# Two value projections as 512-column products, in slabs of four contraction tiles

## The chip, the cores and the metric

The kernel runs on one core of a Trainium2 chip. The metric is the device time of one execution in microseconds (us), given as the median of several runs. The core has five engines that run their own instruction streams and meet only at semaphores: TensorE (PE in the profile; PEld is its weight load), VectorE (DVE), ScalarE (ACT), GpSimd (POOL), and SyncE (SP), which here only issues DMAs.

## The reference

Two transformer blocks on 512 tokens of width 1024, in float32. The change touches only the first block, and there two of the eleven pieces of one input projection:

```
h = rmsnorm(x, g_mix_pre)
proj = h @ w_in                                  # 512 x 1024 times 1024 x N_IN
aq, ak, av, iq, ik, iw, bq, bk, bv, cq, gate_logits = split(proj)
ya = dsa_attention(aq, ak, av, iq, ik, iw, rel_bias) @ w_up_a
yb = stick_breaking_attention(bq, bk, bv) @ w_up_b
yc = memory_attention(cq, mk, mv) @ w_up_c
merged = gates[0]*ya + gates[1]*yb + gates[2]*yc
x = x + rmsnorm(merged @ w_out)
x = x + rmsnorm((silu(h2 @ Wg) * (h2 @ Wu)) @ w_ffn_out)   # h2 = rmsnorm(x)
# then a second block: chunkwise mLSTM layer, dilated window attention, two gated additions
```

`av` and `bv` are both 512 x 512: the value rows (512 tokens by 8 heads of 64). In `dsa_attention` a score per query and key is formed from `iq`, `ik`, `iw`; the 128 best keys of each query are selected, and a softmax over those (8 heads, causal by chunks of 64) weighs the rows of `av`. In `stick_breaking_attention` the weights of `bv`'s rows are exp(log_sigmoid(z) + the sum of log_sigmoid(-z) over later keys).

The kernel runs the three attentions in the order `memory_attention` (the first attention below), `dsa_attention` (the second), `stick_breaking_attention` (the third).

## The kernel before

**Weights in slabs.** All weights come through two slots, each of 2048 words per partition. Slab number g uses slot g mod 2. For each slab SP loads it (`raw`), ScalarE writes a rounded copy (`w_hi`, L1474), GpSimd writes the remainder (`w_lo = raw - w_hi`, L559, or in four quarters, L579), and TensorE multiplies. `split_hi(stage, s)` on ScalarE makes `w_hi` of the slab *after* slab s of the stage; it waits until the slab two before that one has been used. Every product is three matmuls into one accumulator (`mm3`, L734): hi x hi, hi x lo, lo x hi. The stages and the number of slabs of each stand in one table (L50); the semaphore counts `EV_A[stage]` and `EV_V[stage]` say how many evacuations by ScalarE and by VectorE come before a stage.

**The order around the change** is ... `aqk` (4 slabs), `av` (2), `bqk` (4), `bv` (2), `gate` (24). It is written out by hand on each engine. There is no scheduler.

**A 256-column slab** (`gemm_rows`, L853) holds all eight contraction tiles of 256 output columns. With the tokens as the stationary side it makes 4 row tiles x 8 contraction tiles x 3 = 96 matmuls of 256 columns, into two PSUM banks (two row tiles to a bank): banks 0 and 1 for slot 0, banks 2 and 3 for slot 1. When the slab is used up, ScalarE empties one bank and VectorE the other (`to_rows`), each with one 128x512 instruction.

**A wide slab** (`gemm_wide`, L825; used so far only in the second block, by `v2`, `o2` and others) holds four contraction tiles of 512 columns. Two slabs make a group of 512 columns: in the first, all four row tiles take k = 0 to 3, in the second k = 4 to 7, each row tile in a bank of its own. That is 48 matmuls of 512 columns a slab. A row tile is complete only in the second slab; `wait_tile` lets an engine wait for row tile t there (`tile_done`, and `slab_used` for the last one).

**VectorE before the second attention** (L2203 to L2216). VectorE selects the best keys with 96 instructions (`select`, MAX8 and MATCH_REPLACE8 in turn), 20 ahead of each of five evacuations (`aqk` 1 to 3, `av` 0 and 1), but 16 ahead of the last. After the last of them it writes the masks (L2213), then waits for and empties `av` 1. GpSimd waits for the masks (`mask_made`), then writes the offsets (bias plus mask) of unit 0, 1, 2, ... (L644). A unit is one head and one row tile: 32 units.

**The second attention, step by step.** In step n, VectorE forms the negated logits of unit n with their minimum (L2225; needs offset n), and normalises unit n - 1. ScalarE copies transposed probabilities and takes the exponentials of unit n (L1567). TensorE forms the logits of units n and n + 1 in each even step (`pair_logits`, L994), which waits until both logits of the pair before have been read by VectorE (`at_neg`). It fills each of steps 0 to 31 with two of the products of `bqk` (six matmuls, `products_beside`). In step n it transposes unit n - 3 and, in odd steps, multiplies by `av`. ScalarE splits slab 1 of `bqk` at the end of step 1. GpSimd writes its `w_lo` in four quarters, one after each of offsets 2 to 5 (L640 to L648). In steps 33 to 35 TensorE fills with row tile 0 of `bv` (`first_rows_of_bv`, L1021).

**The third attention.** TensorE finishes slab 0 of `bv`, then row tile 0 of slab 1, then the first logits of head 0 (`first_stick_z`), then the rest of slab 1, then the logits of head 1, and so on, one head per step (L1101 to L1132). Head 0 uses banks 2 to 4, head 1 banks 5 to 7, in turn. In step 0, ScalarE and VectorE empty slab 1 of `bv` after their work for head 0.

Of the kernel before, what the change touches and what calls it, by code (L numbers as in the profile page):

```python
# [22 lines left out]
ACT = mybir.ActivationFunctionType  # L23
# [3 lines left out]
P = 128  # L27
S = 512
NT = S // P
D = 1024  # L30
KD = D // P
SLAB = 2048
HALF = 512
# [69 lines left out]

WIDE = {"v2": 2, "o2": 2, "z2": 2, "wout2": 2, "pg0": 2, "kv3": 2, "q3": 3, "wout3": 2, "pg1": 2}
GROUPS = {**{n: 1 for n in WHOLE}, **WIDE}
GROUP_NO = {}
# [119 lines left out]
def _program(nc, A, ctx):  # L226
# [178 lines left out]
    def slot_of(tensor, slot, words=SLAB):  # L405
        return tensor[:, slot * SLAB:slot * SLAB + words]

    def wait_tile(eng, stage, t, c=0):

        if t < NT - 1:  # L410
            eng.wait_ge(tile_done, (NT - 1) * (GROUP_NO[stage] + c) + t + 1)
        else:
            eng.wait_ge(slab_used, BASE[stage] + COUNT[stage] // GROUPS[stage] * (c + 1))
# [23 lines left out]
    def _(sp):  # L437
# [65 lines left out]
        load("aqk", columns(w_in, C_AQ))  # L503
        load("av", columns(w_in, C_AV))
        load("bqk", columns(w_in, C_BQ))
        load("bv", columns(w_in, C_BV))

# [222 lines left out]
    def _(pe):  # L730
# [93 lines left out]

        def gemm_wide(stage, c, x_hi, x_lo, half, kt=KD, ready=None, bank_free=None, between=None, after_tile=None):  # L825

            per = kt // 4
            for s in range(per):
                g = BASE[stage] + per * c + s
                pe.wait_ge(lo_made, g + 1)  # L830
                hi, lo = (slot_of(w, g % 2).rearrange("p (k c) -> p k c", k=4) for w in (w_hi, w_lo))
                if s and between is not None:
                    between()
                for t in range(NT):
                    if s == 0 and bank_free is not None:
                        bank_free(t)
                    for k in range(4 * s, 4 * s + 4):
# [3 lines left out]
                        ins = mm3(banks[:, 4 * half + t, :], x_hi[:, at_], x_lo[:, at_], hi[:, k % 4, :], lo[:, k % 4, :], k == 0, k == kt - 1)  # L841
# [149 lines left out]
        gemm_T("aqk", h_hi, h_lo, first=1, count=3)  # L991
        gemm_rows("av", h_hi, h_lo)

        def pair_logits(n):  # L994

            pe.wait_ge(at_neg, U_A + n)
            for m in (n, n + 1):
                h, t = head_and_tile(m)
                rows = slice(64 * (m % 2), 64 * (m % 2) + 64)
                w = (t + 1) * P  # L1000
                mm(banks[:, 4 + m % 2, 0:w], aqkT[rows, (h // 2) * S + t * P:(h // 2) * S + (t + 1) * P],
                   aqkT[rows, (4 + h // 2) * S:(4 + h // 2) * S + w], True, True).then_inc(at_log, 1)
# [18 lines left out]
        def first_rows_of_bv(k0, k1):  # L1021

            slot = wait_slab("bv", 0, 0, 0)
            hi, lo = (slot_of(w, slot).rearrange("p (k c) -> p k c", k=KD) for w in (w_hi, w_lo))
            for k in range(k0, k1):
                mm3(banks[:, 2 * slot, 0:256], h_hi[:, k * S:k * S + P], h_lo[:, k * S:k * S + P], hi[:, k, :], lo[:, k, :], k == 0, k == KD - 1)
# [64 lines left out]
        def first_stick_z():  # L1091

            pe.wait_ge(at_lo, 8)
            pe.wait_ge(ev_a, EV_A["bv"] + 1)
            pe.wait_ge(ev_v, EV_V["bv"] + 1)
# [352 lines left out]
    def _(act):  # L1448
# [248 lines left out]
        for step in range(8 + 2):  # L1697
# [310 lines left out]
    def _(dve):  # L2008
# [180 lines left out]
        n_select = 2 * (NT - 1) * TOPK // 8  # L2189

        def select(n):

# [10 lines left out]
        n_now = 0  # L2203
        to_empty = [("aqk", s, to_T(aqkT, scale=0.125 if s < 2 else 1.0)) for s in range(1, 4)] + [("av", s, to_rows(av, HALF)) for s in range(2)]
        share = -(-n_select // len(to_empty))
        for n, (stage, s, empty) in enumerate(to_empty):
# [3 lines left out]
            if n_now == n_select:  # L2210
# [23 lines left out]

        each_slab("bv", to_rows(bv, HALF), 0, 1)
        dve.tensor_copy(sums_r[:], sq[:, SQ["ntri"] * P:(SQ["ntri"] + 2) * P]).then_inc(sums_made, 1)
        for step in range(8 + 2):
# [385 lines left out]
```

## Time and profile before

| | us |
|---|---|
| median of 3 runs | 1555.07 (1554.88 to 1556.66) |
| span of the profiled execution, first to last instruction | 1553.7 |
| what the median is above that span | 1.4 |
| PE busy | 1529.0 (98%) |
| DVE, ACT, POOL busy | 703.0, 601.9, 693.8 |

The profile lists no time of the profiled execution apart from its span. TensorE is busy in nearly the whole span and the other four less than half of it. Start times in the rows are microseconds from the start of the span. A matmul's listed duration is its latency: with matmuls in a row, the distance between two starts is what each one costs.

### The profile page before, as it was taken

To read this page: it belongs to the slowest core of one execution; us is meant where nothing else is said; L and a number is where in the kernel's file an instruction comes from. 1 tells how busy PE (TensorE), PEld (TensorE's weight loads), DVE (VectorE), ACT (ScalarE), POOL (GpSimd) and SP (SyncE) were. 2 spreads that over 40 slices of the span, in tenths; PEclk is the share of its full clock that TensorE was granted. 3 is DMA by queue.
4 is the path that set the end of the run, shared out by engine and by line. 5 is a ranking of instruction groups with operands and counts; after the bars stand their busy time and mean duration, and the time that the engine had idled before them with its cause. 6 is when DMAs were issued, how large, how long until landed. Compare 5 with 4: busy or idle time off the path is not lost.

```text
span 1553.7 us, 19713 instructions
## 1 busy us (share of the span) xinstructions
PE 1529.0 (98%) x7588; PEld 1253.4 (81%) x7588; DVE 703.0 (45%) x1147; ACT 601.9 (39%) x916; POOL 693.8 (45%) x312
## 2 busy tenths in 40 slices
PE   8999999999999999999999999999999999999898
PEld 7777967877888888888888888888888888887687
DVE  4258855482334226665654005630034346444733
ACT  6353254673332225122221115422444444355452
POOL 6423455334555535443434444444432435454532
PEclk9999999999999999999999999999999999999999
DMA  7314211102333332433332225543422322222021
GB/s 246 122 55 136 82 55 49 41 21 61 102 101 87 109 109 70 118 97 104 85 108 86 104 82 72 99 104 92 126 68 72 101 89 82 95 82 82 28 72 64
DMA packets 145126, 138.26 MB, mean 89 GB/s; under 512 B 7792, under 2 KB 118384, under 8 KB 145052
## 3 DMA queue, kind: packets, MB, share of 16 engines
q1 hardware_dynamic: 140836, 130.79, 29.3%
q10 hardware_dynamic: 4216, 6.45, 1.3%
q8 instruction: 51, 0.84, 0.2%
q14 instruction: 23, 0.19, 0.0%
HBM read 135.09 MB, written 2.13 MB: 88 GB/s over the span
## 4 chain that ended last, share of the span: by engine, by line
PE 90%; DVE 3%; ACT 3%; POOL 2%; issue 1%; DMA 0%; ACTq 0%; DVEq 0%; POOLq 0%
PE banks L732 87%; PE banks L761 2%; POOL w_lo L579 1%; PE banks L920 1%; PE banks L1350 0%; DVE prob L2552 0%; DVE xs L2072 0%; ACT w_hi L1474 0%; POOL prob L721 0%; DMA vec_rows<-in_norm_a 0%; ACT junk L1523 0%; ACT k L1938 0%; POOL prob L723 0%; ACT junk L1762 0%; DVE head_ms L2514 0%
## 5 line engine op out<-in xcount | busy, mean ns | idle before, releaser
L559 POOL TENSOR_TENSOR w_lo<-raw,w_hi 128x2048 fp32r<-128x2048 f32 x104 | 481.4, 4629 | 602.3 <-ACT w_hi L1474 602.3
L732 PE MATMUL banks<-h_hi,w_hi 128*128 128x512 f32 (+1 forms) x904 | 348.1, 385 | 2.4 <-DVE h_lo L2079 0.9
L732 PE MATMUL banks<-h_hi,w_lo 128*128 128x512 f32 (+1 forms) x904 | 340.4, 377 | 0.0
L732 PE MATMUL banks<-h_lo,w_hi 128*128 128x512 f32 (+1 forms) x904 | 340.1, 376 | 0.0
L1474 ACT ACTIVATE w_hi<-raw 128x2048 fp32r<-128x2048 f32 (+2 forms) x123 | 233.1, 1895 | 213.3 <-PE banks L732 203.1
L732 PEld LDWEIGHTS banks<-h_hi,w_hi 128*128 128x128 f32 x904 | 169.9, 188 | 42.1 <-issue 9.7
L732 PE MATMUL banks<-w_hi,h_hi 128*128 128x512 f32 (+1 forms) x544 | 199.8, 367 | 0.0
L732 PE MATMUL banks<-w_hi,h_lo 128*128 128x512 f32 (+1 forms) x544 | 198.2, 364 | 0.0
L732 PE MATMUL banks<-w_lo,h_hi 128*128 128x512 f32 (+1 forms) x544 | 198.1, 364 | 0.0
L732 PEld LDWEIGHTS banks<-h_hi,w_lo 128*128 128x128 f32 x904 | 169.6, 188 | 32.2
L732 PEld LDWEIGHTS banks<-h_lo,w_hi 128*128 128x128 f32 x904 | 169.9, 188 | 29.5
L579 POOL TENSOR_TENSOR w_lo<-raw,w_hi 128x512 fp32r<-128x512 f32 x84 | 113.6, 1373 | 104.3 <-ACT w_hi L1474 92.1
L732 PEld LDWEIGHTS banks<-w_hi,h_hi 128*128 128x128 f32 x544 | 102.6, 189 | 16.9 <-issue 1.1
L732 PEld LDWEIGHTS banks<-w_hi,h_lo 128*128 128x128 f32 x544 | 102.6, 189 | 16.2
L732 PEld LDWEIGHTS banks<-w_lo,h_hi 128*128 128x128 f32 x544 | 102.7, 189 | 15.8
L2351 DVE TENSOR_TENSOR f_lo<-ff_prod,f_hi 128x512 f32 x22 | 104.2, 4738 | 2.7
L1794 ACT ACTIVATE ff_sig<-banks 128x512 f32<-128x512 f32 x22 | 13.2, 600 | 175.9 <-PE banks L732 175.9
L732 PE MATMUL banks<-w_hi,f_lo 128*128 128x512 f32 x176 | 68.5, 389 | 0.0
L732 PE MATMUL banks<-w_hi,f_hi 128*128 128x512 f32 x176 | 68.5, 389 | 0.0
L732 PE MATMUL banks<-w_lo,f_hi 128*128 128x512 f32 x176 | 68.5, 389 | 0.0
L1735 ACT ACTIVATE gate<-banks,col 128x512 f32<-128x512 f32 x24 | 16.6, 690 | 130.5 <-PE banks L732 130.5
L2060 DVE TENSOR_REDUCE meansq<-sumsq 128x1 f32<-128x2 f32 (+4 forms) x19 | 2.9, 153 | 139.3 <-ACT junk L1762 130.4
(319 smaller groups left out, 2348.6 us busy)
## 6 DMA issues: line engine op xcount, KB each, us to landing
raw<-in_w_in SPq DMA_DIRECT2D x56, 512.0 KB, 4.0
raw<-in_w_ffn_in SPq DMA_DIRECT2D x44, 512.0 KB, 5.0
raw<-in_w_in_a SPq DMA_DIRECT2D x32, 512.0 KB, 5.7
raw<-in_w_ffn_out SPq DMA_DIRECT2D x22, 512.0 KB, 4.0
raw<-in_w_ple_gate SPq DMA_DIRECT2D x16, 512.0 KB, 4.6
raw<-in_w_in_b SPq DMA_DIRECT2D x16, 512.0 KB, 4.5
raw<-in_w_out SPq DMA_DIRECT2D x8, 512.0 KB, 4.0
raw<-in_w_out_a SPq DMA_DIRECT2D x8, 512.0 KB, 4.5
```

The source lines that it names most:

```text
L559: pool.tensor_tensor(slot_of(w_lo, slot), slot_of(raw, slot), slot_of(w_hi, slot).bitcast(F32), ALU.subtract).then_inc(lo_made, 1)
L579: ins = pool.tensor_tensor(w_lo[:, c], raw[:, c], w_hi[:, c].bitcast(F32), ALU.subtract)
L732: return pe.matmul(out, lhsT, rhs, start=start, stop=stop, **kw)
L761: ins = pe.transpose(banks[:, transposed_bank(name, k), t * P:(t + 1) * P], rows(t)[:, k * P:(k + 1) * P], const("ident"))
L920: ins = pe.transpose(banks[:, 6, kt * P:(kt + 1) * P], src[:, kt * P:(kt + 1) * P], const("ident"))
L1474: act.activation(slot_of(w_hi, slot, words), slot_of(raw, slot, words), ACT.Copy).then_inc(hi_made, 1)
L1735: act.activation(gate[slot][:], banks[:, 2 * slot, :], ACT.Sigmoid, bias=col[:, ds(V_BGATE + KD * (s % 3) + ft, 1)]).then_inc(ev_a, 1)
L1794: act.activation(ff_sig[:], banks[:, 2 * slot, :], ACT.Sigmoid).then_inc(ev_a, 1)
L2060: link(dve.tensor_reduce(meansq[:, c], pieces, AX_X, ALU.add))
L2351: dve.tensor_tensor(lo, ff_prod[:], hi.bitcast(F32), ALU.subtract).then_inc(lo_ffn, 1)
```

## The change

Both stages become wide. `av` and `bv` keep two slabs each, now of four contraction tiles by 512 columns. `av` goes to banks 4 to 7 (row tile t in bank 4 + t), `bv` to banks 0, 1, 5 and 6 (`row_bank`). ScalarE empties row tiles 0 and 2, VectorE 1 and 3, so each still runs two 128x512 evacuations per stage.

The waits move with this. VectorE's evacuation between the select blocks now waits for row tile 1 of `av`, which is complete only half-way through slab 1. The first logits of the second attention (banks 4 and 5) wait for row tiles 0 and 1 of `av` to be emptied. The first products of `bv` (bank 0) wait for all of `bqk` to be emptied. The first logits of the third attention come after slab 0 of `bv`. Those of head 1 wait for all of `bv` to be emptied. ScalarE splits the first slab of `gate` after it has emptied `bv`, not before the third attention.

```diff
-WIDE = {"v2": 2, "o2": 2, ...
+WIDE = {"av": 1, "bv": 1, "v2": 2, "o2": 2, ...
+    def row_bank(stage, half, t):
+        return (0, 1, 5, 6)[t] if stage == "bv" else 4 * half + t
-        load("av", columns(w_in, C_AV))
+        load_wide("av", w_in[:, C_AV:C_AV + HALF])
-        load("bv", columns(w_in, C_BV))
+        load_wide("bv", w_in[:, C_BV:C_BV + HALF])
...
 # TensorE
-        gemm_rows("av", h_hi, h_lo)
+        gemm_wide("av", 0, h_hi, h_lo, 1)
         def pair_logits(n):
             pe.wait_ge(at_neg, U_A + n)
+            if n == 0:
+                pe.wait_ge(ev_a, EV_A["av"] + 1)
+                pe.wait_ge(ev_v, EV_V["av"] + 1)
...
         def first_rows_of_bv(k0, k1):
-            slot = wait_slab("bv", 0, 0, 0)
+            wait_emptied(EV_A["bv"], EV_V["bv"])
+            pe.wait_ge(lo_made, BASE["bv"] + 1)
...
-                first_rows_of_bv(*((0, 3), (3, 6), (6, 8))[step - 33])
+                first_rows_of_bv(*((0, 1), (1, 3), (3, 4))[step - 33])
...
-        gemm_rows("bv", h_hi, h_lo, count=1, begun=KD)
-        gemm_rows("bv", h_hi, h_lo, first=1, count=1, between=first_stick_z)
+        gemm_wide("bv", 0, h_hi, h_lo, 0, between=first_stick_z, begun=4)
         for step in range(1, 8 + 2):
             if step < 8:
                 for n, tiles in enumerate(((1, 3, 2), (0,))):
                     if step >= 2:
                         pe.wait_ge(st_a, 2 * (step - 2) + n + 1)
+                    elif n == 0:
+                        wait_emptied(EV_A["gate"], EV_V["gate"])
                     stick_z_mm(step, tiles)
-            if step == 3:
-                pe.wait_ge(ev_a, EV_A["gate"])
-                pe.wait_ge(ev_v, EV_V["gate"])
 # ScalarE
-        each_slab("av", to_rows(av, HALF))
+        split_group("av", 0)
+        wide_rows("av", 1, av)
...
-        each_slab("bv", to_rows(bv, HALF), 0, 1)
-        split_hi(0, "bv", 1)
+        split_hi(0, "bv", 0)
...
             if step == 0:
-                act.wait_ge(slab_used, BASE["bv"] + 2)
-                to_rows(bv, HALF)(0, 1, 1, (BASE["bv"] + 1) % 2)
+                wide_rows("bv", 0, bv)
+                split_hi(0, "bv", 1)
 # VectorE
-        to_empty = [...] + [("av", s, to_rows(av, HALF)) for s in range(2)]
+        to_empty = [...] + [("av", t, None) for t in (1, 3)]
...
-            dve.wait_ge(slab_used, BASE[stage] + s + 1)
-            empty(0, s, s, (BASE[stage] + s) % 2)
+            if stage == "av":
+                wide_rows("av", 1, s, av)
+            else: ...                            # as before
...
             if step == 0:
-                dve.wait_ge(slab_used, BASE["bv"] + 2)
-                to_rows(bv, HALF)(0, 1, 1, (BASE["bv"] + 1) % 2)
+                for t in (1, 3):
+                    wide_rows("bv", 0, t, bv)
```

VectorE ahead of the second attention, before the change. `top_76` and `work` are the selection's tiles; `selected`, `slab_used` and `whole_tile_done` are semaphores.

```order
L2199 MAX top_76<-work 128x8 [waits selected] x2
L2034 COPY av<-banks 128x2x256 [waits slab_used]
L2199 MAX top_76<-work 128x8 [waits selected]
...
L2213 TENSOR_SCALAR masks<-work 128x512
L2034 COPY av<-banks 128x2x256 [waits slab_used]
L2225 ISA prob_117,negmax<-banks,offset_115 128x128 [waits offset_made,probs_T,logits]
```

The same place now:

```order
L2214 MAX top_76<-work 128x8 [waits selected] x2
L2204 COPY av<-banks 128x512 [waits whole_tile_done]
L2214 MAX top_76<-work 128x8 [waits selected]
...
L2228 TENSOR_SCALAR masks<-work 128x512
L2204 COPY av<-banks 128x512 [waits slab_used]
L2243 ISA prob_117,negmax<-banks,offset_115 128x128 [waits offset_made,probs_T,logits]
```

Nothing has changed its place: the copy stands ahead of the last 16 selects as before, but it waits for another event.

TensorE in step 33 of the second attention, before: nine matmuls of `bv` (`w_hi`, `w_lo` against `h_hi`, `h_lo`), the transposes of unit 30 (`prob_119`), the products by `av`.

```order
L732 MATMUL banks<-w_hi,h_hi 128x256 [waits lo_made,emptied_by_vector,emptied_by_scalar]
L732 MATMUL banks<-w_lo,h_hi 128x256
L732 MATMUL banks<-w_hi,h_lo 128x256
...
L920 MATMUL banks<-sq,prob_119 128x128 [waits probs_T_copied,probs]
L920 MATMUL banks<-sq,prob_119 128x128 x3
L732 MATMUL banks<-probT_121,av 64x128 [waits probs_T_copied]
```

And now:

```order
L736 MATMUL banks<-w_hi,h_hi 128x512 [waits lo_made,emptied_by_vector,emptied_by_scalar]
L736 MATMUL banks<-w_lo,h_hi 128x512
L736 MATMUL banks<-w_hi,h_lo 128x512
L924 MATMUL banks<-sq,prob_119 128x128 [waits probs_T_copied,probs]
L924 MATMUL banks<-sq,prob_119 128x128 x3
L736 MATMUL banks<-probT_121,av 64x128 [waits probs_T_copied]
```

Three wide matmuls stand where nine narrow ones stood. The semaphores have the same names, but the count waited for is now one higher: it takes in the last slab of `bqk`.

## Rows read from the trace of the kernel before

**Rows 1.** The page: busy time by engine, and the granted clock in 40 slices.

```profile
PE 1529.0 (98%) x7588; PEld 1253.4 (81%) x7588; DVE 703.0 (45%) x1147; ACT 601.9 (39%) x916; POOL 693.8 (45%) x312
...
PEclk9999999999999999999999999999999999999999
```

**Rows 2.** Waits of TensorE from 150 to 320 us: who waited for whom, total, times, longest.

```profile
PE banks L732 <- ACT stick_a L1717: 0.7, 2, 0.5
```

**Rows 3.** Timeline of ScalarE: start, duration, engine, line, operation, idle time before.

```profile
154.13 0.60 ACT L1493 ACTIVATE aqkT<-banks 128x512 f32<-128x512 f32 x1 [8.48 <-PE banks L732]
...
165.01 0.60 ACT L1493 ACTIVATE aqkT<-banks 128x512 f32<-128x512 f32 x1 [8.47 <-PE banks L732]
...
176.52 0.60 ACT L1501 ACTIVATE av<-banks 128x512 f32<-128x512 f32 x1 [9.11 <-PE banks L732]
...
188.04 0.60 ACT L1501 ACTIVATE av<-banks 128x512 f32<-128x512 f32 x1 [9.12 <-PE banks L732]
...
189.76 1.90 ACT L1474 ACTIVATE w_hi<-raw 128x2048 fp32r<-128x2048 f32 x1
```

**Rows 4.** Timeline of ScalarE in `v2`, a wide stage: row tiles 0 and 2.

```profile
1047.35 0.60 ACT L1833 ACTIVATE v<-banks 128x512 f32<-128x512 f32 x1 [0.74 <-PE banks L732]
1052.79 0.60 ACT L1833 ACTIVATE v<-banks 128x512 f32<-128x512 f32 x1 [4.84 <-PE banks L732]
```

**Rows 5.** Timeline of VectorE around the end of `av`; then units 3 and 5.

```profile
177.13 0.68 DVE L2199 MAX8 top<-work 128x8 f32<-128x512 f32 x1
...
185.34 0.90 DVE L2213 TENSOR_SCALAR masks<-work 128x256 f32<-128x256 f32 x3
188.04 0.69 DVE L2034 COPY av<-banks 128x512 f32<-128x512 f32 x1 [1.80 <-PE banks L732]
188.65 0.28 DVE L2225 CUSTOM_DVE_ANT_0 prob<-banks,offset 128x128 f32<-128x128 f32 x1
...
193.89 0.42 DVE L2225 CUSTOM_DVE_ANT_0 prob<-banks,offset 128x256 f32<-128x256 f32 x1 [0.78 <-POOL offset L644]
...
198.41 0.56 DVE L2225 CUSTOM_DVE_ANT_0 prob<-banks,offset 128x384 f32<-128x384 f32 x1 [1.03 <-POOL offset L644]
```

**Rows 6.** Timeline of TensorE: logits of the pairs 0, 2, 4 and 6.

```profile
187.93 0.49 PE L732 MATMUL banks<-aqkT 64*128 64x128 f32 x4
...
191.30 0.70 PE L732 MATMUL banks<-aqkT 64*128 64x256 f32 x4
...
195.02 0.92 PE L732 MATMUL banks<-aqkT 64*128 64x384 f32 x4
...
199.70 1.13 PE L732 MATMUL banks<-aqkT 64*128 64x512 f32 x4
```

**Rows 7.** Timeline of GpSimd: the first offsets and the first quarter of `w_lo`.

```profile
186.32 0.87 POOL L644 TENSOR_TENSOR offset<-bias,masks 128x128 f32<-128x128 f32 x2 [2.70 <-DVE masks L2213]
...
191.73 1.29 POOL L579 TENSOR_TENSOR w_lo<-raw,w_hi 128x512 fp32r<-128x512 f32 x1 [1.99 <-ACT w_hi L1474]
```

**Rows 8.** Timeline of TensorE in steps 33 to 35, where `bv` begins.

```profile
266.56 0.36 PE L732 MATMUL banks<-w_hi,h_hi 128*128 128x256 f32 x1
...
267.71 0.60 PE L920 MATMUL banks<-sq,prob 128*128 128x128 f32 x4
...
271.51 1.09 PE L732 MATMUL banks<-probT,av 128*64 128x128 f32 x16
```

**Rows 9.** Timeline of ScalarE: the last evacuation of `bqk`.

```profile
267.23 0.59 ACT L1493 ACTIVATE bqkT<-banks 128x512 f32<-128x512 f32 x1
```

**Rows 10.** Timeline of TensorE: the end of `bv`, then the logits of head 1.

```profile
295.21 0.28 PE L732 MATMUL banks<-w_hi,h_lo 128*128 128x256 f32 x1
295.42 2.42 PE L732 MATMUL banks<-bqkT 64*128 64x384 f32 x8
```

**Rows 11.** Timeline of VectorE: the last evacuation of `bv`.

```profile
295.53 0.69 DVE L2034 COPY bv<-banks 128x512 f32<-128x512 f32 x1 [0.89 <-PE banks L732]
```

**Rows 12.** Timeline of ScalarE: the first work on head 1.

```profile
297.02 1.46 ACT L1706 ACTIVATE stick_a<-banks 128x768 f32<-128x768 f32 x2 [0.90 <-PE banks L732]
```

More of the change, by code:

```diff
@@ L101 @@
 PIECES = {"post": 2, "fpost": 2, "g0": 2, "kv3": 2, "g1": 2}
-WIDE = {"v2": 2, "o2": 2, "z2": 2, "wout2": 2, "pg0": 2, "kv3": 2, "q3": 3, "wout3": 2, "pg1": 2}
+WIDE = {"av": 1, "bv": 1, "v2": 2, "o2": 2, "z2": 2, "wout2": 2, "pg0": 2, "kv3": 2, "q3": 3, "wout3": 2, "pg1": 2}
 GROUPS = {**{n: 1 for n in WHOLE}, **WIDE}
@@ L823, in gemm_T, with gemm_wide @@
             slabs_after(after, stage, body, first, count)
-        def gemm_wide(stage, c, x_hi, x_lo, half, kt=KD, ready=None, bank_free=None, between=None, after_tile=None):
+        def gemm_wide(stage, c, x_hi, x_lo, half, kt=KD, ready=None, bank_free=None, between=None, after_tile=None, begun=0):
             per = kt // 4
@@ L836, in gemm_wide @@
                         bank_free(t)
-                    for k in range(4 * s, 4 * s + 4):
+                    for k in range(max(4 * s, begun if t == 0 else 0), 4 * s + 4):
                         if t == 0 and ready is not None:
@@ L840, in gemm_wide @@
                         at_ = slice(k * S + t * P, k * S + (t + 1) * P)
-                        ins = mm3(banks[:, 4 * half + t, :], x_hi[:, at_], x_lo[:, at_], hi[:, k % 4, :], lo[:, k % 4, :], k == 0, k == kt - 1)
+                        ins = mm3(banks[:, row_bank(stage, half, t), :], x_hi[:, at_], x_lo[:, at_], hi[:, k % 4, :], lo[:, k % 4, :], k == 0, k == kt - 1)
                     if s == per - 1 and t < NT - 1:
@@ L1021, in first_rows_of_bv @@
         def first_rows_of_bv(k0, k1):
-            slot = wait_slab("bv", 0, 0, 0)
-            hi, lo = (slot_of(w, slot).rearrange("p (k c) -> p k c", k=KD) for w in (w_hi, w_lo))
+            wait_emptied(EV_A["bv"], EV_V["bv"])
+            pe.wait_ge(lo_made, BASE["bv"] + 1)
+            hi, lo = (slot_of(w, BASE["bv"] % 2).rearrange("p (k c) -> p k c", k=4) for w in (w_hi, w_lo))
             for k in range(k0, k1):
-                mm3(banks[:, 2 * slot, 0:256], h_hi[:, k * S:k * S + P], h_lo[:, k * S:k * S + P], hi[:, k, :], lo[:, k, :], k == 0, k == KD - 1)
+                mm3(banks[:, 0, :], h_hi[:, k * S:k * S + P], h_lo[:, k * S:k * S + P], hi[:, k, :], lo[:, k, :], k == 0, False)
         for step in range(32 + LAG_OUT):
@@ L1093, in first_stick_z @@
             pe.wait_ge(at_lo, 8)
-            pe.wait_ge(ev_a, EV_A["bv"] + 1)
-            pe.wait_ge(ev_v, EV_V["bv"] + 1)
             stick_z_mm(0, (1, 3, 2))
             stick_z_mm(0, (0,))
-        gemm_rows("bv", h_hi, h_lo, count=1, begun=KD)
-        gemm_rows("bv", h_hi, h_lo, first=1, count=1, between=first_stick_z)
+        gemm_wide("bv", 0, h_hi, h_lo, 0, between=first_stick_z, begun=4)
         for step in range(1, 8 + 2):
@@ L1673, in _, with wide_rows @@
         each_slab("aqk", to_T(aqkT), 2, 2)
-        each_slab("av", to_rows(av, HALF))
+        def wide_rows(stage, half, dst):
+            for t in (0, 2):
+                wait_tile(act, stage, t)
+                act.activation(dst[:, t * HALF:(t + 1) * HALF], banks[:, row_bank(stage, half, t), :], ACT.Copy).then_inc(ev_a, 1)
+        split_group("av", 0)
+        wide_rows("av", 1, av)
         empty_a = {("bqk", s): to_T(bqkT, scale=0.125 if s < 2 else 1.0) for s in range(4)}
@@ L2189, in _, with wide_rows @@
         n_select = 2 * (NT - 1) * TOPK // 8
+        def wide_rows(stage, half, t, dst):
+            wait_tile(dve, stage, t)
+            dve.tensor_copy(dst[:, t * HALF:(t + 1) * HALF], banks[:, row_bank(stage, half, t), :]).then_inc(ev_v, 1)
         def select(n):
@@ L2203, in _ @@
         n_now = 0
-        to_empty = [("aqk", s, to_T(aqkT, scale=0.125 if s < 2 else 1.0)) for s in range(1, 4)] + [("av", s, to_rows(av, HALF)) for s in range(2)]
+        to_empty = [("aqk", s, to_T(aqkT, scale=0.125 if s < 2 else 1.0)) for s in range(1, 4)] + [("av", t, None) for t in (1, 3)]
         share = -(-n_select // len(to_empty))
@@ L2214, in _ @@
                 ins.then_inc(mask_made, 1)
-            dve.wait_ge(slab_used, BASE[stage] + s + 1)
-            empty(0, s, s, (BASE[stage] + s) % 2)
+            if stage == "av":
+                wide_rows("av", 1, s, av)
+            else:
+                dve.wait_ge(slab_used, BASE[stage] + s + 1)
+                empty(0, s, s, (BASE[stage] + s) % 2)
         empty_a = {("bqk", s): to_T(bqkT, scale=0.125 if s < 2 else 1.0) for s in range(4)}
@@ L2233, in _ @@
             beside(BESIDE_A, step, empty_a)
-        each_slab("bv", to_rows(bv, HALF), 0, 1)
         dve.tensor_copy(sums_r[:], sq[:, SQ["ntri"] * P:(SQ["ntri"] + 2) * P]).then_inc(sums_made, 1)
```

## The prediction

> **What bounds the kernel now.** I read the page first: TensorE is busy in 98% of the span [rows 1]. Whatever shortens TensorE's own stream is worth its full length, and whatever makes it wait costs its full length. I then read who TensorE waits for between 150 and 320 us, where both changed stages lie. The longest total is 0.7 us in two waits [rows 2], so there is almost no slack to give back. The question is then what a 256-column matmul costs against a 512-column one, and which of the new waits TensorE reaches too early. For the second I follow the timelines of all engines at the two seams.
>
> **Narrow against wide.** ScalarE's evacuations mark the ends of slabs. A slab of 48 matmuls of 512 columns takes 165.01 - 154.13 = 10.88 us (227 ns each), one of 96 matmuls of 256 columns 188.04 - 176.52 = 11.52 us (120 ns each) [rows 3]. In the wide stage `v2`, row tiles 0 and 2 are complete 5.44 us apart [rows 4], which is half of 10.88: wide products with tokens as the stationary side run at the same rate. Each of the four slabs loses 0.64 us: **-1.28 us for `av`, -1.28 us for `bv`**. These 2.56 us are the whole gain.
>
> The row says that each matmul costs 107 ns per 256 columns plus 13 ns. The Trainium skill, in "TensorE: Matmul & The Clock Gate", section "Back-to-back issue gap", gives N / 2.4 + 2.5 ns. By the page the 192 matmuls that go would be worth only 0.5 us in place of 2.6, and my time would be 2.1 us higher. The measured distances decide here.
>
> SP issues four DMAs per stage as before, and ScalarE and VectorE run the same number of 128x512 evacuations. I cost these at nothing: the slabs are loaded and split a slab ahead.
>
> **Seam 1: the start of the second attention.** VectorE's chain before it is: empty part of `av`, 16 selects, masks, empty the rest, first logits. Before, the first of these started when slab 0 of `av` was used up, at 176.52. The 16 selects ran from 177.13 and the masks ended at 186.24, which released GpSimd's first offset at 186.32 [rows 5, 7]. The last evacuation was still waiting for TensorE, until 188.04: the masks were done 1.8 us early.
>
> Now the 20 selects before it still end at about 176.3, but VectorE waits for row tile 1, complete in slab 1. The stage begins at 187.84 - 2 x 11.52 = 164.80 (187.84 being the end of the narrow matmuls, just ahead of the logits at 187.93 [rows 6]). Row tile 1 is complete at 164.80 + 10.88 + 5.44 = 181.12. With the same 0.2 us to the start of the copy, VectorE starts at 181.35 and the selects at 181.95, 4.8 us later than before. The masks end at 191.05 and the offsets begin at 191.14. VectorE idles 5 us in between, and has no other work there.
>
> From here I shift the events of before:
> - The first negated logits of unit 0 can follow offset 0 (191.14 + 0.44), at 191.6; they were at 188.65 [rows 5]. Those of unit 1 follow offset 1 (192.01) and are read by 192.4.
> - TensorE is through with `av` at 186.6 instead of 187.84, does the logits of pair 0 and the products of steps 0 and 1, and reaches the logits of pair 2 at 190.0 (before: 191.30 [rows 6]). It waits for unit 1 until 192.45. That is 1.15 us later than before.
> - ScalarE takes the exponentials of units 0 and 1 and only then splits slab 1 of `bqk`: at 192.85 in place of 189.76 [rows 3], 3.09 us late. Queued behind that are the exponentials of unit 2. GpSimd's first quarter of `w_lo` waits for this split: before, it started at 191.73, just after the split [rows 7]. Offsets 3, 4 and 5 stand behind the quarters in GpSimd's queue, without idle time in between, so all move by 3.09 us.
> - Unit 3 of VectorE was released by its offset at 193.89, unit 5 at 198.41 [rows 5]. They now come at 196.98 and 201.5. TensorE's logits of pair 4 need unit 3, those of pair 6 unit 5. Before, TensorE came to them 0.65 us (195.02 against 194.37) and 0.7 us (199.70 against 199.0) after the release. So pair 4 starts at 197.5, **2.5 us later than before**. Pair 6 is 2.4 us late by its offset, so it costs nothing more. From there VectorE and GpSimd again have idle time, and TensorE does not recover what it lost.
>
> Net of seam 1, with the gain of `av` inside: +2.5 us. From both sides: if GpSimd's quarters and offsets catch up, only the wait for pair 2 is left, +1.15; if no slack helps, +3.1. I take 2.5, because the releases by the offset stand in the rows.
>
> **Seam 2: the start of `bv`.** In before's times, without the shift. At 266.56 TensorE began `bv` in step 33 [rows 8], into banks 2 and 3. It now writes bank 0, where the last slab of `bqk` lies. ScalarE empties that from 267.23 to 267.82 [rows 9], behind its copy for the unit before. TensorE waits until 267.87: +1.31. Queued behind are the transposes of unit 30, the products by `av` and ScalarE's next copy, which waits for those products; all move along. Step 33 now fills with three wide matmuls (0.79 us) where nine narrow ones took 1.15 (266.56 to 267.71); step 34 has six for nine, and step 35 three for six, where TensorE waits for the copy anyway. The products by `av` of step 35 start at 272.78 instead of 271.51: +1.27. The rest of `bv`, 84 wide for 168 narrow matmuls, brings back 84 x 13 ns = 1.1. It ends 0.1 to 0.2 us later than before; I take **+0.1 us**. The gain of `bv` and this wait cancel.
>
> If ScalarE's evacuation were in time, this wait would cost 0; it can't exceed 1.3.
>
> **Seam 3: the logits of head 1.** They came right behind the last product of `bv` at 295.42 [rows 10], since their banks were free. Now they use banks that hold row tiles 2 and 3 of `bv`. VectorE can start on row tile 3 about 0.1 us after TensorE is done and needs 0.69 [rows 11]. TensorE, done at 295.5 with the 0.1 of seam 2, goes on at 296.35: **+0.85 us**. ScalarE's first work on head 1 (297.02 [rows 12]) moves along, and its chain sets the pace of this attention: TensorE's waits there are on ScalarE [rows 2]. The bounds are 0.7 (the copy) and 1.0. The earlier start of head 0 hides nothing, since TensorE is busy with `bv` meanwhile. ScalarE's later split of the first `gate` slab ends near 295 and GpSimd's `w_lo` near 300, ahead of the first masking by GpSimd at 302; I cost it at 0.
>
> **Sum.** +2.5 + 0.1 + 0.85 = +3.45 us. The span becomes 1553.7 + 3.5 = 1557.2, the time 1.4 us above it. From the median of the runs: 1555.07 + 3.45 = **1558.5 us**. With all bounds: 1.15 - 1.2 + 0.7 = +0.6 (seam 2's wait absent) and 3.1 + 0.2 + 1.0 = +4.3, and +5.6 if wide products here brought only half of what the rows say.
>
> **The rivals.**
> - *A, not slower: the gain shows in full at the first seam.* If VectorE's selection were ready when `av` ends, as it was before by 1.8 us, the seam would give -1.28; with the waits at `bv` hidden as well the time is 1555.07 - 2.56 = 1552.5 (with them, 1554.7). It decides at the masks: they would have to end before 188. For it speaks that VectorE is only 45% busy. Against it: 9.1 us of selects and masks stand behind a wait that ends at 181.35, by rows of exactly these instructions.
> - *B, the delays are partly absorbed.* GpSimd or ScalarE catch up within the first steps, or the evacuation of `bqk` is in time. Then +0.5 to +2.5, about 1556.7. For it: slacks of 0.65 us that I could misjudge. Against it: GpSimd has no idle time in that stretch.
> - *C, more than the sum.* A gap of 2.4 us in TensorE is longer than any in these rows, and the granted clock, in full in every slice [rows 1], could fall behind it. At the lower of the two levels, 1.2 in place of 2.4 GHz, each microsecond of matmul work takes two, so a stretch of 2.4 us would cost 1.2 to 2.4 more: some 1560.5. The Trainium skill ("TensorE: Matmul & The Clock Gate", section "What's actually happening") says that the clock is throttled after idling and released by activity; no row here shows it at work.
>
> **How the numbers follow.** Forecast 0.62 (own range 1557.3 to 1559.5), A 0.08, B 0.20, C 0.10. The range: C and half of A may lie outside, so 1555.0 to 1560.0. What a measurement of this kernel can tell from no change is 0.2%, 3.1 us: slower means above 1558.2. Of the forecast three quarters lie there (0.45), and all of C: slower 0.55. Even the full gain of 2.56 us is less than 0.2%, so most of A, all of B and a quarter of the forecast count as the same: 0.42. Faster 0.03.
>
> **What would show it.** Right: VectorE idle for 5 us before its copy of `av`; masks ending 3 us after the logits of pair 0 could start; TensorE idle twice, about 2.4 and 1.3 us, ahead of pairs 2 and 4; 1.3 us ahead of the first `bv` product; 0.9 us ahead of head 1, with a VectorE copy as the releaser; slabs of `av` 10.88 us long. Wrong: TensorE without idle time at step 2, slabs that take 11.5 us, or waits elsewhere, as for a slab's `w_lo`.

## The result, and the profile after

The changed kernel takes 1560.07 us (median of 8 runs, 1558.49 to 1563.02). The kernel before, run again 8 times beside it, takes 1556.14 (1554.88 to 1558.40). The ratio is 1.0028, with a 95% interval of 1.0019 to 1.0037: slower by 3.9 us. The profiled spans are 1558.3 us after and 1553.7 before.

The page answers to [rows 1]. TensorE's busy time fell by 1.8 us and its matmuls by 192, yet the span is 4.6 us longer, so TensorE stood still for longer.

```profile
span 1558.3 us, 19326 instructions
...
PE 1527.2 (98%) x7396; PEld 1242.8 (80%) x7396; DVE 703.8 (45%) x1147; ACT 601.7 (39%) x916; POOL 693.7 (45%) x312
...
PEclk9999999999999999999999999999999999999999
```

Where it stood still is in the waits of TensorE from 150 to 325 us (total, times, longest). Three lines head the list; of before, the longest total was 0.7 [rows 2].

```profile
PE banks L736 <- DVE negmax L2243: 3.6, 2, 2.4
PE banks L736 <- ACT bqkT L1497: 1.1, 1, 1.1
PE banks L736 <- DVE bv L2204: 0.9, 1, 0.9
PE banks L736 <- ACT stick_a L1727: 0.6, 2, 0.4
```

The timeline of TensorE, to be read against [rows 6, 8, 10], gives their places: the logits of pairs 0, 2, 4 and 6, the first product of `bv`, the logits of head 1.

```profile
187.75 0.49 PE L736 MATMUL banks<-aqkT 64*128 64x128 f32 x4
...
193.61 0.70 PE L736 MATMUL banks<-aqkT 64*128 64x256 f32 x4 [2.43 <-DVE negmax L2243]
...
198.60 0.92 PE L736 MATMUL banks<-aqkT 64*128 64x384 f32 x4 [1.21 <-DVE negmax L2243]
...
203.28 1.13 PE L736 MATMUL banks<-aqkT 64*128 64x512 f32 x4
...
271.45 0.50 PE L736 MATMUL banks<-w_hi,h_hi 128*128 128x512 f32 x1 [1.07 <-ACT bqkT L1497]
...
300.20 0.99 PE L736 MATMUL banks<-bqkT 64*128 64x384 f32 x3 [0.87 <-DVE bv L2204]
```

The chain behind the first two waits starts in VectorE's timeline [rows 5]. It idles 5.06 us before its copy of row tile 1, and the masks end at 192.14 (191.24 + 0.90), 4.4 us behind TensorE, which had its last product of `av` done by 187.75.

```profile
182.42 0.69 DVE L2204 COPY av<-banks 128x512 f32<-128x512 f32 x1 [5.06 <-PE banks L736]
...
191.24 0.90 DVE L2228 TENSOR_SCALAR masks<-work 128x256 f32<-128x256 f32 x3
192.05 0.68 DVE L2204 COPY av<-banks 128x512 f32<-128x512 f32 x1
192.85 0.29 DVE L2243 CUSTOM_DVE_ANT_0 prob<-banks,offset 128x128 f32<-128x128 f32 x1
...
198.11 0.42 DVE L2243 CUSTOM_DVE_ANT_0 prob<-banks,offset 128x256 f32<-128x256 f32 x1 [2.94 <-POOL offset L648]
```

ScalarE [rows 3] splits slab 1 of `bqk` at 193.99, behind the late exponentials, and GpSimd [rows 7] holds the offset of unit 3 behind a quarter of that slab's `w_lo`. This sets the second wait.

```profile
166.10 0.60 ACT L1497 ACTIVATE aqkT<-banks 128x512 f32<-128x512 f32 x1 [8.48 <-PE banks L736]
...
179.70 0.60 ACT L1682 ACTIVATE av<-banks 128x512 f32<-128x512 f32 x1 [0.74 <-PE banks L736]
...
185.14 0.60 ACT L1682 ACTIVATE av<-banks 128x512 f32<-128x512 f32 x1 [4.84 <-PE banks L736]
...
193.99 1.90 ACT L1478 ACTIVATE w_hi<-raw 128x2048 fp32r<-128x2048 f32 x1
```

```profile
192.22 1.74 POOL L648 TENSOR_TENSOR offset<-bias,masks 128x128 f32<-128x128 f32 x3 [8.58 <-DVE masks L2228]
...
195.97 1.29 POOL L583 TENSOR_TENSOR w_lo<-raw,w_hi 128x512 fp32r<-128x512 f32 x1 [2.01 <-ACT w_hi L1478]
197.22 0.72 POOL L648 TENSOR_TENSOR offset<-bias,masks 128x256 f32<-128x256 f32 x1
```

**A common clock for the traces.** The last evacuation of `aqkT` is ahead of everything the change touches in TensorE's stream. It starts at 165.01 before [rows 3] and at 166.10 after: 1.09 us of the 4.6 arise in code that both kernels share. Below I call this evacuation the anchor, and measure from it to the first ScalarE activation of the `gate` stage (358.19 before, 362.88 after), which lies behind everything changed. From there to the end all traces need 1195.4 to 1195.6 us. The `gate` activation, before and after:

```profile
358.19 0.69 ACT L1735 ACTIVATE gate<-banks,col 128x512 f32<-128x512 f32 x1
```

```profile
362.88 0.69 ACT L1745 ACTIVATE gate<-banks,col 128x512 f32<-128x512 f32 x1
```

The distance is 193.18 us before and 196.78 after: **+3.60 us is what the change costs in the traces.** Of this, +2.49 is reached by the logits of pair 4 (30.01 behind the anchor before, 32.50 after) and +1.11 in the rest.

### The profile page after: what moved, and what is told of

Read it like the earlier page. It is cut to its first block, busy times and chain, and to the rows that moved or that the text cites. A ratio compares the mean times of both kernels' runs of the same rounds, so it can differ in the third digit from the quotient of the medians.

```text
span 1558.3 us, 19326 instructions
## 1 busy us (share of the span) xinstructions
PE 1527.2 (98%) x7396; PEld 1242.8 (80%) x7396; DVE 703.8 (45%) x1147; ACT 601.7 (39%) x916; POOL 693.7 (45%) x312
## 4 chain that ended last, share of the span: by engine, by line
PE 89%; DVE 4%; ACT 3%; POOL 2%; issue 1%; DMA 0%; ACTq 0%; DVEq 0%; POOLq 0%
PE banks L736 85%; PE banks L765 2%; POOL w_lo L583 1%; PE banks L924 1%; ACT w_hi L1478 0%; PE banks L1354 0%; DVE prob L2569 0%; DVE xs L2082 0%; DMA vec_rows<-in_norm_a 0%; POOL prob L725 0%; DVE work L2216 0%; ACT junk L1527 0%; ACT k L1948 0%; POOL prob L727 0%; ACT junk L1772 0%
## 5 line engine op out<-in xcount | busy, mean ns | idle before, releaser
L736 PE MATMUL banks<-w_hi,h_hi 128*128 128x512 f32 x480 | 188.6, 393 | 1.1 <-ACT bqkT L1497 1.1
L736 PE MATMUL banks<-w_hi,h_lo 128*128 128x512 f32 x480 | 186.9, 389 | 0.0
L736 PE MATMUL banks<-w_lo,h_hi 128*128 128x512 f32 x480 | 186.8, 389 | 0.0
L736 PEld LDWEIGHTS banks<-w_hi,h_hi 128*128 128x128 f32 x480 | 90.1, 188 | 20.5 <-ACT bqkT L1497 1.3
L736 PEld LDWEIGHTS banks<-w_hi,h_lo 128*128 128x128 f32 x480 | 90.1, 188 | 18.7
L736 PEld LDWEIGHTS banks<-w_lo,h_hi 128*128 128x128 f32 x480 | 90.2, 188 | 18.2
```

The costliest lines, as they stand in the source:

```text
L736: return pe.matmul(out, lhsT, rhs, start=start, stop=stop, **kw)
```

## The experiments

There are eleven runs in three groups: the two kernels once more, and nine new ones. Each is timed in five rounds against the kernel before, whose medians in the groups are 1555.89, 1555.65 and 1556.23. "Trace" is the change in the anchor-to-`gate` distance against 193.18.

### Is it the change, or the execution? Both kernels once more

No edit. `before_again`: 

> The kernel before, unchanged, timed against itself, to see what moves by itself. In the changed kernel's trace everything is already 1.09 us later than in before's when TensorE takes up its first product (12.87 against 11.78 us), because the first vec_rows transposes waited 3.0 us for a DMA and not 2.0. Theory S (start noise): this wait varies from run to run with the same code, so here too the first product starts somewhere between 11.7 and 13, and the two medians differ by up to 1 us. Rival (the changed code starts later): here it starts at 11.8 within 0.1 us, and the ratio is 1.0000 within 0.0003.

`after_again`: 

> The changed kernel, unchanged. Theory S: measured from the first product (11.78 us in before's trace) to the end of the span the difference to before is +3.5 us as in the first trace, wherever the first product starts; the ratio of times is 1.0022 within its interval. Rival (the changed code starts later): the first product starts at 12.9 again, and the ratio is 1.0029.

Before: 1555.95 us, ratio 0.9999 (0.9990 to 1.0008), trace 0.00. After: 1559.29 us, 1.0019 (1.0010 to 1.0028), trace +3.53. The cost repeats to 0.07 us, and is +3.4 by this group's medians. The anchor moved by 0.27 in the unchanged kernel and stayed at 166.04 in the changed one, though its first product came early this time. From the first product, as theory S wanted to measure, the difference between the two kernels would be +4.6, not +3.5. So the detail of that theory was wrong: the late start isn't one wait. These rows of TensorE's start show two waits on DMAs that differ from run to run, of the first profile of the changed kernel

```profile
9.40 0.28 PE L883 MATMUL banks<-sq,vec_rows 32*128 32x32 f32 x1 [3.04 <-DMA vec_rows<-in_norm_a]
...
25.95 0.67 PE L736 MATMUL banks<-root_diag,sq 128*128 128x256 f32 x2 [0.20 <-DMA sq<-in_c_sq]
```

and of the second:

```profile
8.13 0.28 PE L883 MATMUL banks<-sq,vec_rows 32*128 32x32 f32 x1 [1.66 <-DMA vec_rows<-in_norm_a]
...
26.40 0.67 PE L736 MATMUL banks<-root_diag,sq 128*128 128x256 f32 x2 [1.13 <-DMA sq<-in_c_sq]
```

The nine kernels that follow, all with changed code, had the anchor at 164.51 to 165.81, on both sides of before. So the 1.09 us can't be put down to the change.

### One stage at a time: `av_only`, `bv_only`

```diff
-WIDE = {"av": 1, "bv": 1, "v2": 2, ...}
+WIDE = {"av": 1, "v2": 2, ...}    # av_only: loads, banks, waits and evacuations of bv as before
+WIDE = {"bv": 1, "v2": 2, ...}    # bv_only: those of av as before
```

`av_only`: 

> Only av is wide; bv, its banks, its waits and its evacuations are as in before. The seams' theory: +2.5 us over before, all of it made between the last product of aqk and the logits of pair 4, with waits of TensorE of 2.4 and 1.2 us on VectorE; nothing of it comes back. Rival (the loss is in bv, the delay of the softmax is absorbed by the slack of its 32 steps): -1.3 to 0.

`bv_only`: 

> Only bv is wide; av, its banks and VectorE's selection are as in before. The seams' theory: +1.0 us over before: -2 x 0.64 for the wide slabs, +1.1 to 1.3 for the wait on ScalarE's last bqk evacuation, +0.9 to 1.0 for the wait on VectorE's last bv evacuation. Rival (ScalarE's chain in the third attention hides what comes before it): -1.3 to -0.3.

`av` alone: 1558.42 us, 1.0017 (1.0007 to 1.0026), trace +2.68. `bv` alone: 1557.18 us, 1.0008 (0.9999 to 1.0017), trace +1.11. The two add up to 3.79 against 3.60 together. The waits of `bv_only` are those of seams 2 and 3:

```profile
PE banks L736 <- ACT bqkT L1494: 1.1, 1, 1.1
PE banks L736 <- DVE bv L2200: 0.9, 1, 0.9
```

`av_only` held a surprise: only one wait at seam 1 is listed, and still it costs the full sum. The windows (length, then busy time and count of PE, PEld, DVE, ACT, POOL, then the granted clock, the DMA share and GB/s) show why. This is `av_only` just behind its 2.43 us gap

```profile
192.00:197.00 5.00, 3.83 (x12) 2.67 (x13) 2.13 (x11) 3.19 (x7) 2.85 (x5) 0.66 0.01 3
```

and this is the changed kernel in the same stretch, behind the same gap:

```profile
192.00:197.00 5.00, 3.39 (x17) 2.54 (x17) 2.58 (x12) 3.35 (x8) 2.62 (x4) 1.00 0.01 3
```

The clock, at 2.4 GHz in full, fell for part of the stretch to 1.2 GHz: windows of 1 us show it at 0.50 from 193 to 196. In `av_only` the products behind the gap are 0.42 us apart and from 197.3 on again 0.23:

```profile
193.17 1.23 PE L736 MATMUL banks<-aqkT 64*128 64x256 f32 x4 [2.43 <-DVE negmax L2247]
...
194.92 0.63 PE L736 MATMUL banks<-h_lo,w_hi 128*128 128x512 f32 x1
195.34 0.63 PE L736 MATMUL banks<-h_hi,w_lo 128*128 128x512 f32 x1
...
197.33 0.39 PE L736 MATMUL banks<-h_hi,w_lo 128*128 128x512 f32 x1
197.56 0.39 PE L736 MATMUL banks<-h_hi,w_hi 128*128 128x512 f32 x1
...
198.33 0.92 PE L736 MATMUL banks<-aqkT 64*128 64x384 f32 x4
```

TensorE works slowly through the time in which it would have waited for unit 3. So a lower clock is nearly free here: pair 4 starts 32.68 us behind the anchor, 0.18 later than in the changed kernel.

### Undo the late masks: `masks_first`

All selects and the masks come ahead of VectorE's wait for row tile 1, in the time in which it idled; both stages stay wide.

```diff
-            while n_now < min(n_select, share * (n + 1)):
+            while n_now < (n_select if n >= 3 else share * (n + 1)):
...
-            if n_now == n_select:
+            if n == 3:
```

> The changed kernel, except that VectorE runs all remaining 36 selects and the masks ahead of its copy of row tile 1 of av, not 16 selects and the masks behind it. Seams' theory: VectorE no longer idles for 5 us, the masks end near 185.5 in before's times, row tile 1 is emptied by 186.1, ahead of the logits of pair 0 at 186.65, and the two waits before pairs 2 and 4 go. Seam 1 gives back its 3.8 us: 1.28 of gain for av is left there, and with +1.1 of the bv seams the kernel is 0.2 us faster than before (between -0.5 and +0.2). Rival (TensorE waits at the start because pair 0 needs the evacuated banks 4 and 5, whatever VectorE does with the masks): the copy now comes 4 us later than in the changed kernel, so it stays as slow, or becomes slower.

Measured: 1555.76 us, 1.0007 (0.9996 to 1.0019), trace -0.20. Both waits on `negmax` are gone and those at `bv` stay:

```profile
PE banks L736 <- ACT bqkT L1497: 1.1, 1, 1.1
PE banks L736 <- DVE bv L2204: 0.9, 1, 0.9
PE banks L736 <- ACT stick_a L1727: 0.7, 2, 0.5
```

Pair 4 starts 28.73 us behind the anchor, 1.28 before [rows 6]: the gain of wide products in `av` exactly as its price was worked out. What seam 1 lost is the masks' order alone. The rival is out: the copy of row tile 1 comes 4 us later, and TensorE still doesn't wait at the start of the attention.

### How much lateness does it take? `dose28`, `dose24`

The changed kernel does 80 of the 96 selects ahead of the wait for row tile 1, `masks_first` all 96. These do 88 and 84.

```diff
-            while n_now < min(n_select, share * (n + 1)):
+            while n_now < (min(n_select, (20, 40, 60, 60 + 28, n_select)[n])):   # dose24: 60 + 24
```

`dose28`: 

> 28 selects ahead of the copy of row tile 1 of av, 8 behind it: the masks end 3.95 us earlier than in the changed kernel (177.13 to 181.08 in before's trace), near 187.1 in before's times. Seams' theory: both releases come before TensorE arrives (pair 4 by only 0.2 us), no wait is left, and the kernel is as fast as the one with the masks first: 3.8 us below the changed kernel, -0.2 against before. Rival (only an early copy and masks that are done when the logits start help): something between the two.

`dose24`: 

> The changed kernel with 24 selects ahead of VectorE's copy of row tile 1 of av and 12 behind it (20 and 16 in the changed kernel, 36 and 0 in the kernel with the masks first). Four selects take 2.18 us in before's trace (177.13 to 179.31), so the masks end 2.18 us earlier. Seams' theory: the wait ahead of pair 2 shrinks from 2.4 to about 0.3 us, since TensorE arrives where it did and the release comes 2.2 us earlier; the wait ahead of pair 4 does not shrink but stays near 1.3 us, because TensorE now arrives 2.2 us earlier too and GpSimd's offset 3 still follows the late split. Seam 1 is +0.3 over before, and the kernel 2.2 us faster than the changed one. Rival (one wait, proportional to how late the masks are): the wait ahead of pair 4 shrinks as well, or vanishes first.

With 88: 1556.31 us, 1.0009 (0.9996 to 1.0022), trace -0.15, no wait on `negmax`. With 84: 1557.04 us, 1.0007 (0.9998 to 1.0017), trace +1.39. TensorE in `dose24`, the logits of pairs 0, 2 and 4:

```profile
186.84 0.49 PE L736 MATMUL banks<-aqkT 64*128 64x128 f32 x4
...
190.54 0.70 PE L736 MATMUL banks<-aqkT 64*128 64x256 f32 x4 [0.26 <-DVE negmax L2243]
...
195.53 0.92 PE L736 MATMUL banks<-aqkT 64*128 64x384 f32 x4 [1.21 <-DVE negmax L2243]
```

The trace of `dose24` is 2.21 us below that of the changed kernel, where 2.2 was expected. Two microseconds of lateness less take the first wait from 2.43 to 0.26 and leave the second whole; two more take both away. By time the steps can't be told apart, by trace they can.

### Cut the second wait alone: `split_early`

ScalarE splits slab 1 of `bqk` ahead of the attention, not behind the exponentials of units 0 and 1.

```diff
+        split_hi(0, "bqk", 0)
         for step in range(32 + LAG_OUT):
...
             for stage, s in slabs_begun(slabs, step):
-                split_hi(0, stage, s)
+                if (stage, s) != ("bqk", 0):
+                    split_hi(0, stage, s)
```

> The changed kernel, except that ScalarE splits slab 1 of bqk ahead of the exponentials of unit 0, in the 7 us in which it idles, and not behind those of unit 1. Seams' theory: the masks stay late, and so does the 2.4 us wait ahead of pair 2, but GpSimd's quarter of w_lo no longer waits; offset 3 comes 2 us earlier, and the 1.2 us wait ahead of pair 4 goes: 1.2 us faster than the changed kernel where the clock holds. Where the granted clock falls behind the 2.4 us gap (as in the trace of the kernel with only av wide, 0.66 over 5 us), the slow matmuls are no longer covered by the second wait, and cost up to 1.2 us: then about the same as the changed kernel. Rival (the second wait is for the late logits alone): no difference at all.

Measured: 1558.78 us, 1.0022 (1.0013 to 1.0032), trace +3.28. The wait before pair 4 is gone, the one before pair 2 stays:

```profile
192.38 0.70 PE L736 MATMUL banks<-aqkT 64*128 64x256 f32 x4 [2.43 <-DVE negmax L2245]
...
196.09 0.92 PE L736 MATMUL banks<-aqkT 64*128 64x384 f32 x4
```

GpSimd's quarter follows its offsets without a gap, where in the changed kernel it had waited 2.01 us for the split:

```profile
190.99 1.74 POOL L648 TENSOR_TENSOR offset<-bias,masks 128x128 f32<-128x128 f32 x3 [8.58 <-DVE masks L2230]
192.69 1.29 POOL L583 TENSOR_TENSOR w_lo<-raw,w_hi 128x512 fp32r<-128x512 f32 x1
193.93 0.73 POOL L648 TENSOR_TENSOR offset<-bias,masks 128x256 f32<-128x256 f32 x1
```

Pair 4 is at 31.22 behind the anchor, 1.28 earlier than in the changed kernel, but at `gate` only 0.32 of it is left. The rest went at seam 3, where the clock fell in this run. Granted clock in the columns as above:

```profile
295.00:305.00 10.00, 9.12 (x38) 7.08 (x37) 2.66 (x5) 6.66 (x9) 4.51 (x1) 0.83 0.27 74
```

The changed kernel shows 1.00 there. Windows of 1 us put the fall at 300 to 304 us (0.58, 0.50, 0.50, 0.71). Of the nine timed runs of this kernel, four have a mean clock of 0.998 or less, which none of the kernel before's 93 runs in these groups shows, and the median run is one of them. The other five are at 0.999, and so are runs of the kernel before, so their clock says nothing. The time can't be set against that of a kernel at full clock. The mechanism of the second wait is shown by the trace; its price in time is not.

### Other banks for `bv`: `seam3_only`, `banks`

`seam3_only` gives row tiles 1 and 2 the banks 5 and 6, so that head 1 needs banks that are emptied earlier. `banks` also moves row tile 0 away from `bqk`'s last bank.

```diff
-        return (0, 1, 5, 6)[t] if stage == "bv" else 4 * half + t
+        return (0, 5, 6, 1)[t] if stage == "bv" else 4 * half + t    # seam3_only
+        return (5, 6, 0, 1)[t] if stage == "bv" else 4 * half + t    # banks
...
                     elif n == 0:
-                        wait_emptied(EV_A["gate"], EV_V["gate"])
+                        wait_emptied(EV_A["bv"] + 2, EV_V["bv"] + 1)    # banks: EV_A["bv"] + 1
...
+            if step == 3:
+                wait_emptied(EV_A["gate"], EV_V["gate"])
```

In `banks` the first products of `bv` wait for `at_neg, U_A + 32`, and the wait for the evacuations of `bqk` stands ahead of the rest of the stage.

`seam3_only`: 

> The changed kernel, except that row tiles 1, 2 and 3 of bv go to banks 5, 6 and 1: row tile 0 stays in bank 0, where the last slab of bqk lies, and the logits of head 1 no longer wait for row tile 3. Seams' theory: the 1.1 us wait on ScalarE's bqk evacuation stays, the 0.9 us wait on VectorE's last bv evacuation goes: 0.9 us off the changed kernel. Rival (the third attention starts when ScalarE is ready): nothing comes off.

`banks`: 

> The changed kernel, except that row tiles 0 to 3 of bv go to banks 5, 6, 0, 1 and not 0, 1, 5, 6. Row tile 0 then needs only that the logits of unit 31 have been read, long before; all of bqk has to be emptied only for row tiles 2 and 3, after step 35; the logits of head 1 wait for row tiles 0 and 1 alone. Seams' theory: both waits of the bv seams go, 1.1 and 0.9 us, and 2.1 to 2.3 us come off the changed kernel: +1.2 over before. Rival (ScalarE's own chain in the third attention sets its start): only the first wait's 1.1 us comes off.

`seam3_only`: 1558.47 us, 1.0015 (1.0006 to 1.0024), trace +2.76. `banks`: 1557.18 us, 1.0011 (1.0002 to 1.0020), trace +1.80. The first lost the wait on `bv` and won 0.84 against the changed kernel's +3.60; the second lost both and won 1.80, less than the 2.1 to 2.3 that were expected. The difference lies at seam 1: in `banks` the clock fell behind the gap there as in `av_only` (0.66 from 192 to 197), which cost 0.28 at pair 4. From pair 4 to `gate`, `banks` is 2.08 us shorter than the changed kernel. Each seam costs about what its wait says (0.84 for 0.87, 2.08 for 1.07 and 0.87 together), and each can be taken away by itself.

### The version without the three seams: `all_three`

The edits of `masks_first` and `banks` together.

> Masks first and the new bank order together: wide slabs without any of the waits. Seams' theory: what is left is the price of narrow against wide, 4 x 0.64 = 2.56 us faster than before (ratio 0.9984, -2.2 to -2.8), no wait of TensorE longer than 0.5 us between 150 and 320 us except those of before. Rival (the page's 2.5 ns per matmul, and the 13 ns seen are something else): -0.5 us.

Measured: 1553.14 us (1552.57 to 1556.44), 0.9988 (0.9979 to 0.9996), trace -2.19. It is 2.5 us faster than the kernel before by this group's medians, and by the medians of the two groups 5.9 us faster than the changed kernel (3.4 + 2.5). In the trace it is at the edge of what was expected (2.2 to 2.8), and the rival's -0.5 is out. No new wait is left; the kernel before has these same three:

```profile
PE banks L736 <- ACT stick_a L1730: 0.7, 2, 0.5
PE banks L736 <- POOL stick_a L620: 0.6, 1, 0.6
PE banks L736 <- DVE sp_hi L2275: 0.2, 1, 0.2
```

The masks end at 185.06, 1.4 us ahead of the logits of pair 0 at 186.42:

```profile
184.16 0.90 DVE L2231 TENSOR_SCALAR masks<-work 128x256 f32<-128x256 f32 x3
184.97 0.68 DVE L2207 COPY av<-banks 128x512 f32<-128x512 f32 x1
```

So the gain of the wide products is real, and the change as made lost it, and more, to waits at three seams that aren't inherent in it.

## Why the prediction was right in its mechanism and wrong in its range

The forecast was 1558.5 with a range up to 1560.0; the time is 1560.07, just outside. The change itself was forecast at +3.45 and measured +3.93 by medians, +3.40 in the repeat, +3.60 and +3.53 in the traces. By its own steps:

- **The base, where it failed.** "1555.07 + 3.45": the first term is the median of three runs. Eight runs beside the changed kernel gave 1556.14, and the three groups 1555.65 to 1556.23. The base was 1.07 too low, more than twice what the change was mis-sized by (0.48, by medians), and the two make up the 1.55 between forecast and result. The range had no term for it: its working took in the bounds of the seams and left the spread of the base at nothing, although the three runs themselves lay 1.8 us apart (1554.88 to 1556.66), and the anchor alone moves by 1.6 us between executions (164.51 to 166.10). The range also ended below two of its own cases, the bound of +5.6 (1560.7) and rival C (1560.5).
- **What the 0.48 is.** Of the changed kernel's first 8 runs, the four at a mean clock of 1.000 have a median of 1559.5, 3.4 above before, as in the repeat. The other 0.5 comes in with the four runs at 0.998 (see rival C).
- **Narrow against wide.** For `av` -1.28 was forecast; `masks_first` shows -1.28 at pair 4, and `all_three` -1.27. Right. For `bv` -1.28 was too much. `all_three`, without waits, brings 2.19 - 1.27 = 0.92. Measured from the anchor, it is 1.27 ahead of before at the first product of `bv` (100.28 against 101.55), 1.16 ahead at the products by `av` of step 35 (105.34 against 106.50), and 2.19 ahead at the logits of head 1 (128.22 against 130.41). So the twelve wide products in steps 33 to 35 bring nothing (they lose 0.11; step 35 takes 0.93 us from its first `bv` product on in both kernels, with three wide products for six narrow), and the 84 behind them bring 1.03 for the 1.1 of seam 2's working. The Trainium skill ("TensorE: Matmul & The Clock Gate", section "Back-to-back issue gap") gives its N / 2.4 + 2.5 ns for an isolated matmul. By it all four slabs together bring 0.5 us, and these traces don't agree: `all_three` brings 2.19.
- **Seam 1.** +2.5 against +2.49. The two waits were forecast at 2.4 and 1.3 and are 2.43 and 1.21; VectorE idles 5.06 for 5; unit 3 comes from the offset behind the quarter. `masks_first` and the doses show the masks as the cause, `split_early` the split as what passes it on to pair 4. The delay by the quarters was the step most in doubt, and it held. One sign of the prediction was a slip: it has the masks end 3 us after pair 0 could start, while its own times (191.05 and 186.6) make that 4.4, which is what was measured.
- **Seam 2.** The start of `bv` was forecast 1.31 late. In `bv_only` it is 102.86 behind the anchor against 101.55, so 1.31 late, and the products by `av` of step 35 are 1.28 late (107.78 against 106.50) for 1.27. The 1.07 in the list of waits is shorter, because it counts from the end of the transposes ahead of it, and before, the first product started 0.25 behind the start of these transposes. With the smaller gain of `bv` the net at head 1 is +0.21 for +0.1 (`seam3_only`: +2.70 there, of which 2.49 are seam 1's).
- **Seam 3.** The logits of head 1 were forecast 0.85 late; they are 0.99 late (+3.69 in the changed kernel against +2.70 in `seam3_only`), with VectorE's copy as the releaser, and 0.84 of it is left at `gate`. So the forecast of the sum is near the mark partly by luck: at head 1 the two `bv` seams cost 1.20 for 0.95, and 0.1 of that is won back behind it.
- **Rival A** is what `all_three` does: 2.5 us under before by medians and 2.19 in the trace, where A gave 2.56. Its condition, masks done before 188, was the right one. In before's times they end at 187.1 in `dose28`, without a wait, and at 188.9 in `dose24`, with one of 0.26. The kernel as changed doesn't meet it.
- **Rival B** is out: nothing was absorbed. With 84 selects ahead of the wait (`dose24`) it would have been near the time.
- **Rival C** got a chance of 0.10 and a price of 1.2 to 2.4 us. The fall is real (0.66 over 5 us in `av_only` and in `banks`), but in neither profile of the changed kernel, and behind the gap of seam 1 it cost 0.2 to 0.3 us, since the second wait takes it in. At seam 3 of `split_early`, with no such wait behind it, it cost 0.96. Half of the changed kernel's 8 runs have a mean clock of 0.998; three of these are its slowest (1560.9, 1562.59, 1563.02) and one its fastest (1558.49), so the clock can't be the whole of it. The repeat's runs at 0.998 to 0.999 are no slower than its others (1558.54 to 1559.99). What made the three slow ones is open: they weren't profiled. The experiments show that single runs can lose far more than C's price. In the 93 runs of the kernel before in the three groups the mean clock is never below 0.999 and no time is above 1558.24, but seven runs of `bv_only`, `masks_first`, `split_early`, `dose24` and `dose28` have a clock of 0.992 to 0.995 and take 1560.3 to 1565.87 us. All five kernels have both waits at `bv`. `banks`, `all_three`, `av_only` and `seam3_only`, which lack at least one of them, have no run below 0.998, but neither has the changed kernel, which has both. Where the clock falls in the seven runs isn't shown. The Trainium skill ("TensorE: Matmul & The Clock Gate", section "What's actually happening") has the clock throttled after idling; these traces agree that it happens, and add that the same 2.43 us gap does it in one execution and not in another.

## What to carry to other kernels

When TensorE is the bound, the price of each matmul is the easy part: ask of every engine what it did between the old release and the new one, since work queued behind a wait that comes later is late by the whole difference (here masks, then offsets, then a split), though the engine idles just before. Work that needs nothing of the new result goes ahead of the wait, and new banks are chosen by who needs them next. And an effect of 3 us is forecast against a base that itself moves by 1: give the base a term in the range, and measure inside the trace from a common event.

## What was not expected of the hardware

- **The clock isn't the same from execution to execution.** Behind the 2.43 us gap it was 0.66 over 192 to 197 us in `av_only` and `banks`, and 1.00 in both profiles of the changed kernel. In `split_early` it stayed 1.00 behind that gap and was 0.83 over 295 to 305, where TensorE's wait is only 0.9 us and ends at 297.64, 2 to 3 us ahead of the fall.
- **The start varies.** TensorE's waits on its first DMAs (0.73 to 3.04 us for `vec_rows`, 0 to 1.78 for the `sq` read from `in_c_sq`) move the anchor by up to 1.6 us, in code that is the same in all kernels.
